# Loading the first expert's first weight pair elsewhere, and writing out its products ahead of the loop

## The chip, the cores and the metric

The kernel runs on one core of a Trainium2 chip. The time is that of one execution on the device, in microseconds (us); it is the median of several runs. A profiled execution gives the trace that all rows below come from.

Names of engines: PE is TensorE's matmuls and PEld its weight loads, DVE is VectorE, ACT is ScalarE, POOL is GpSimd, SP is SyncE, which here only issues transfers (DMAs). A "q" behind a name (PEldq, SPq) is the engine's instruction queue.

## What is computed

A decoder block on 512 tokens of 1024 channels: a Conformer convolution branch and a sliding-window attention branch, merged by gates and added to x, then a mixture of experts and a final norm. Only the mixture matters here:

```python
logits = (t @ w_router + b_router).astype(F32)
top_val, top_idx = lax.top_k(logits, TOP_K)        # 4 of 32 experts for each token
gate = jax.nn.softmax(top_val, axis=-1)
...
def expert_block(args):
    xb, e = args
    h = xb @ w_mlp1[e] + b_mlp1[e]                 # 1024 -> 2048
    glu, lin = jnp.split(h, 2, axis=-1)
    glu = jnp.minimum(glu, SWIGLU_LIMIT)
    lin = jnp.clip(lin, -SWIGLU_LIMIT, SWIGLU_LIMIT)
    a = glu * jax.nn.sigmoid(SWIGLU_ALPHA * glu) * (lin + 1)
    return a @ w_mlp2[e] + b_mlp2[e]               # 1024 -> 1024
```

The 32 experts' weights are 402 MB of float32, each read once.

## The kernel before

It has three blocks one after the other, with a barrier of all engines between them: `dense_half` (norm, projections, convolution, attention, output projection, second norm u2, router and lists), `mixture` (the experts) and `finish` (the last sum and norm).

**Places in SBUF.** `big` holds an expert's weights: `t.w1` is its first 16384 columns, eight slots of 2048 columns, one for each 128 rows of w_mlp1; two slots are a *pair*, 2 MB, and there are four pairs. `t.w2` is the rest, loaded as two halves of 2 MB. There is one place for each, no second buffer. `xT` holds the normed rows `t.u2` at the end of `dense_half`, and `t.early[0]` at the end of the mixture; between them it is not used.

**Loads in `dense_half`** (SP's queue, lines 214 to 229). When the merge is done: x (line 215), pairs 0 to 2 of expert 0 (line 219), both halves of its w2 (line 221). When the output projection is done: pair 3 (line 224), whose place held an operand of it. Then the four parts of u2 are written out to memory as they come (line 228), since the mixture gathers each expert's tokens from there, and SP waits for them (line 229).

**The expert loop.** Experts are taken from a list made on the chip: a piece is up to 96 tokens. TensorE (lines 1170 to 1178) loads the piece's token count, and branches: over 64 tokens it runs `work` with three groups of 32 tokens, else with two. In the trace expert 0 has three groups and expert 1 two. `work` does the products of slots 0 to 3 for all groups, with the finding of the tokens (`dispatch`) of the expert after the next between them, then slots 4 to 7 group by group, then the products with w2 (`down`). After the last use of a pair it raises `s_w1used`, after that of a half of w2 `s_w2used`.

SP (lines 965 to 974) loads the next expert's weights, in the order pair 0 to 3, then w2's halves. Each waits until TensorE has used the same place for the expert before: pair 0 of expert 1 can be issued only when TensorE has used pair 0 of expert 0. POOL issues the gather of an expert's tokens (`xg`, line 986) and the scatter of its result (line 1006).

**Ahead of the loop in `mixture`.** TensorE dispatches expert 0, adds the gated biases to h (line 174), dispatches expert 1 and turns expert 0's gathered tokens (line 1076). SP issues the final norm's weights (line 964).

Of the kernel before, what the change touches and what calls it, by code (L numbers as in the profile page):

```python
# [30 lines left out]
P = 128  # L31
D = 1024
SEQ = 512
TT = SEQ // P
# [12 lines left out]
E = 32  # L47
# [3 lines left out]
NG = CAP // G  # L51
K_EACH = 4
PAIRS = KB // 2
FC = 256
# [103 lines left out]
def halves(ap, n):  # L158
    return ap.rearrange("p (a n) -> p a n", n=n)
# [23 lines left out]
def dense_half(nc, t):  # L183
# [5 lines left out]
    with nc.Block() as block:  # L189

        @block.sync
        def _(sp):
# [24 lines left out]
            sp.wait_ge(t.s_merge, 2 * KB)  # L217
            for q in range(PAIRS - 1):
                sp.dma_start(t.w1[:, 2 * q:2 * q + 2, :], t.d_w1[0, q]).then_inc(t.s_w1[q], 16)
# [6 lines left out]
            for j in range(TT):  # L226
                sp.wait_ge(t.s_u2, j + 1)
                sp.dma_start(t.d_u2[j * P:(j + 1) * P, :], t.u2[:, j, :]).then_inc(t.s_u2out, 16)
            sp.wait_ge(t.s_u2out, 16 * TT)

        @block.gpsimd
# [710 lines left out]
def mixture(nc, t):  # L942
# [8 lines left out]
    with nc.Block() as block:  # L951
# [7 lines left out]
        @block.sync  # L959
        def _(sp):  # L960
            n = piece_count(sp)
            last = sp.value_load(t.lists[0:1, P + 1:P + 2], min_val=E - 1, max_val=E + MORE - 1)

            sp.dma_start(t.gfin[:, :], t.d_gfin.partition_broadcast(P)).then_inc(t.s_fin, 16)
            with sp.Fori(1, n) as i:
                e = expert_of(sp, i)
                for q in range(PAIRS):
                    sp.wait_ge(t.s_w1used, i * PAIRS + (q + 1 - PAIRS))
                    sp.dma_start(t.w1[:, 2 * q:2 * q + 2, :], t.d_w1[bass.ds(e, 1), q].rearrange("e p a n -> (e p) a n")).then_inc(t.s_w1[q], 16)
                for q in range(2):  # L970
                    sp.wait_ge(t.s_w2used, i * 2 + (q - 1))
                    sp.dma_start(t.w2[:, 2 * q:2 * q + 2, :, :],
                                 t.d_w2[bass.ds(e, 1), q].rearrange("e p j a n -> (e p) j a n")).then_inc(t.s_w2[q], 16)

            sp.wait_ge(t.s_scat, last * 16)
            for r in range(TOPK - 1):
                if r:
                    sp.wait_ge(t.s_w1used, last * PAIRS + r)
                sp.dma_start(t.early[r], t.d_y4[:, :, r, :]).then_inc(t.s_early[r], 16)
# [67 lines left out]
        def _(pe):  # L1047
# [30 lines left out]

            def up(k, g):

                for c in range(4):
                    cols = t.w1[:, k, :].rearrange("p (a n) -> p a n", a=2)[:, :, c * FC:(c + 1) * FC]
                    mm = pe.matmul(halves(bank[g][c * G:(c + 1) * G, :], FC), t.xe[:, k, PLACE[g]:PLACE[g] + G], cols,  # L1083
                                   start=(k == 0), stop=(k == KB - 1), tile_position=(0, c * G))
                return mm
# [33 lines left out]

            def work(i, groups):  # L1120

                last = groups - 1
                for k in range(K_EACH):
                    if k % 2 == 0:
                        pe.wait_ge(t.s_w1[k // 2], i * 16 + 16)
                    for g in range(groups):
                        mm = up(k, g)
                    if k % 2:
# [6 lines left out]
                for g in range(groups):  # L1135
# [3 lines left out]
                    for k in range(K_EACH, KB):  # L1139
                        if g == 0 and k % 2 == 0:  # L1140
                            pe.wait_ge(t.s_w1[k // 2], i * 16 + 16)
                        mm = up(k, g)
                        if g == last and k % 2:
# [25 lines left out]
            pe.wait_ge(t.s_acc, 2 * TT)  # L1169
            with pe.Fori(0, n) as i:  # L1170
                pe.wait_ge(t.s_xe, i * 2 + 2)
# [3 lines left out]
                with pe.If(tokens > (NG - 1) * G):  # L1175
                    work(i, NG)
                with pe.Else():
                    work(i, NG - 1)

# [155 lines left out]
def build(nc, io):  # L1335
    with ExitStack() as ctx:
# [54 lines left out]
        t.xT = halves(xT[:, :], SEQ)  # L1391
        t.u2 = halves(xT[:, :], D)
        t.early = (t.u2, halves(big[:, 0:4096], D), halves(big[:, 4096:8192], D))
        t.o_lo = halves(xT_r[:, :], SEQ)
# [258 lines left out]
```

## Time and profile before

| what | value |
|---|---|
| median of 3 runs | 1584.43 us (1584.23 to 1585.93) |
| profiled execution | 1582.41 us |
| its span, first to last instruction | 1580.6 us |
| mean granted TensorE clock | 0.967 of full speed |
| busy: PE, DVE, ACT, POOL | 90%, 47%, 36%, 22% of the span |
| moved | 475 MB, 301 GB/s on average, about 425 GB/s in the expert loop |

Times in rows are counted from the span's start. A matmul's busy time is modelled and overlaps its neighbours', so PE's 90% is not a measure of how full it is. The DMA share is the mean of the core's 16 DMA engines; 1.00 means that there was always something to move. "issue" as a releaser means that an engine waited for nothing that the profile shows.

### The profile page before, as it was taken

To read this page: it belongs to the slowest core of one execution; us is meant where nothing else is said; L and a number is where in the kernel's file an instruction comes from. 1 tells how busy PE (TensorE), PEld (TensorE's weight loads), DVE (VectorE), ACT (ScalarE), POOL (GpSimd) and SP (SyncE) were. 2 spreads that over 40 slices of the span, in tenths; PEclk is the share of its full clock that TensorE was granted. 3 is DMA by queue.
4 is the path that set the end of the run, shared out by engine and by line. 5 is a ranking of instruction groups with operands and counts; after the bars stand their busy time and mean duration, and the time that the engine had idled before them with its cause. 6 is when DMAs were issued, how large, how long until landed. Compare 5 with 4: busy or idle time off the path is not lost. (4 is left out here: it accounts for less than half of the span.)

```text
span 1580.6 us, 35484 instructions
## 1 busy us (share of the span) xinstructions
PE 1428.3 (90%) x13353; PEld 762.1 (48%) x13354; DVE 742.3 (47%) x1786; ACT 567.0 (36%) x1078; POOL 346.5 (22%) x229
## 2 busy tenths in 40 slices
PE   5999999799997689999999999999889898999991
PEld 2788776566776234433344434434333433344341
DVE  6699977899214623422233332333323422323236
ACT  3444444755223023422333332432323333224233
POOL 4578777411551000000000000000000000000000
PEclk9999999899999799999999999999999999999995
DMA  4222221111329189999999999999999999999995
GB/s 155 84 93 94 92 94 64 44 41 41 114 92 409 64 326 389 429 427 416 387 374 428 419 430 426 419 428 428 428 427 422 429 409 425 427 388 407 426 412 219
DMA packets 51665, 475.18 MB, mean 301 GB/s; under 512 B 9136, under 2 KB 9392, under 8 KB 27056
## 3 DMA queue, kind: packets, MB, share of 16 engines
q1 hardware_dynamic: 42000, 455.71, 70.4%
q0 software_dynamic: 8480, 16.79, 2.8%
q10 hardware_dynamic: 1152, 2.24, 0.4%
q8 instruction: 20, 0.33, 0.1%
q14 instruction: 13, 0.11, 0.0%
HBM read 471.56 MB, written 16.78 MB: 309 GB/s over the span
## 5 line engine op out<-in xcount | busy, mean ns | idle before, releaser
L1083 PE MATMUL bank<-big,ring 128*32 128x512 f32 x4992 | 568.1, 601 | 44.0 <-issue 22.1
L1083 PEld LDWEIGHTS bank<-big,ring 128*32 128x32 f32 x4992 | 152.3, 111 | 382.2 <-issue 347.9
L1109 PE MATMUL bank<-big,mix 128*32 128x256 f32 x4992 | 288.6, 382 | 3.9 <-DMA big<-in_d_w 3.8
L1109 PEld LDWEIGHTS bank<-big,mix 128*32 128x32 f32 x4992 | 164.1, 110 | 98.8 <-DMA big<-in_d_w 7.4
L1042 ACT ACTIVATE mix<-bank,sgate 32x256 f32<-32x256 f32 x384 | 178.7, 465 | 67.1 <-PE bank L1109 42.9
L986 POOL DMA_INDIRECT ring<-u_rows,gidx x34 | 34.4, 1010 | 580.0 <-PE bank L1076 567.0
L1030 ACT ACTIVATE ring<-ring 128x256 f32<-128x256 f32 x96 | 40.0, 416 | 312.7 <-DVE ring L1236 312.7
L474 PE MATMUL bank<-mix_r,sm_r 128*128 128x512 f32 x328 | 132.9, 405 | 17.3 <-POOL uT_r L247 10.8
L1027 ACT ACT_TABLE_LOAD x32 | 41.1, 1283 | 262.9 <-PE bank L1067 262.9
L474 PE MATMUL bank<-mix_r,ring_r 128*128 128x512 f32 x344 | 135.0, 392 | 0.0
L474 PE MATMUL bank<-uT_r,sm_r 128*128 128x512 f32 x328 | 128.7, 392 | 0.0
L719 DVE SCALAR_TENSOR_TENSOR bank<-big,chan,bank 128x512 f32<-128x512 f32 x176 | 116.6, 748 | 0.0
L1006 POOL DMA_INDIRECT y_rows<-mix,sidx x32 | 29.8, 932 | 378.0 <-ACT mix L1042 378.0
L242 POOL TENSOR_TENSOR ring_r<-ring,sm_r 128x1024 fp32r<-128x1024 f32 x41 | 100.6, 2454 | 54.0 <-ACT sm_r L316 53.2
L1201 DVE COPY slot<-bank 128x9 f32<-128x9 f32 x34 | 5.7, 169 | 203.7 <-PE bank L1059 203.7
L1247 DVE COPY mix<-bank 128x256 f32<-128x256 f32 x96 | 40.6, 423 | 116.1 <-PE bank L1095 116.1
L1234 DVE TENSOR_TENSOR ring<-bank,b 128x512 f32<-128x512 f32 x96 | 65.6, 684 | 53.3 <-PE bank L1083 52.5
L1219 DVE COPY lT<-kf 128x128 f32 x33 | 7.5, 227 | 160.5 <-PE bank L1067 155.4
L474 PEld LDWEIGHTS bank<-mix_r,sm_r 128*128 128x128 f32 x328 | 62.4, 190 | 36.4 <-issue 10.4
L474 PEld LDWEIGHTS bank<-mix_r,ring_r 128*128 128x128 f32 x344 | 65.5, 190 | 14.4 <-issue 1.4
L474 PEld LDWEIGHTS bank<-uT_r,sm_r 128*128 128x128 f32 x328 | 62.2, 190 | 13.3
L1191 DVE TENSOR_SCALAR mix<-kb,first,place 128x480 bf16<-128x480 bf16 x136 | 45.9, 401 | 22.1 <-issue 20.3
(272 smaller groups left out, 1753.2 us busy)
## 6 DMA issues: line engine op xcount, KB each, us to landing
big<-in_d_w SPq DMA_DIRECT2D x192, 2048.0 KB, 18.4
ring<-in_d_dense SPq DMA_DIRECT2D x67, 512.0 KB, 3.2
big<-y_rows SPq DMA_DIRECT2D x2, 2048.0 KB, 19.6
xT<-in_d_xT SPq DMA_DIRECT2D x4, 512.0 KB, 9.3
uT<-in_d_x SPq DMA_DIRECT2D x1, 2048.0 KB, 9.8
u_rows<-xT SPq DMA_DIRECT2D x4, 512.0 KB, 16.6
xT<-y_rows SPq DMA_DIRECT2D x1, 2048.0 KB, 12.8
xT<-y_rows SPq DMA_DIRECT2D x4, 512.0 KB, 5.4
```

What stands on the lines that cost most here:

```text
L242: pool.tensor_tensor(t.wlo[:, slot, :], t.wring[:, slot, :], hi.bitcast(F32), ALU.subtract).then_inc(t.s_wlo, 1)
L474: mm = pe.matmul(out, a, b, start=start and i == 0, stop=stop and i == 2)
L719: conv.add(dve.scalar_tensor_tensor(row if k == TAPS_V - 1 else acc, tap(k), weight(k), acc, ALU.mult, ALU.add))
L986: pool.indirect_dma_start(out=t.xg[:, :], out_offset=None, in_=t.d_u2, in_offset=bass.IndirectOffsetOnAxis(ap=t.gidx[:, 0:1], axis=0), bou ...
L1027: act.activation(t.b1[:, half * FC:(half + 1) * FC], bank[PY[half]][:, FC:], ACT.Copy).then_inc(t.s_b1, 1)
L1030: act.activation(t.sig[:, g, :], t.hb[:, g, 0:FC], ACT.Sigmoid, scale=ALPHA).then_inc(t.s_sig, 1)
L1042: out = act.activation(t.ysb[PLACE[g]:PLACE[g] + G, c * FC:(c + 1) * FC], bank[PY[g % 2]][token, 0:FC], ACT.Copy, scale=t.sgate[token, bas ...
L1083: mm = pe.matmul(halves(bank[g][c * G:(c + 1) * G, :], FC), t.xe[:, k, PLACE[g]:PLACE[g] + G], cols, start=(k == 0), stop=(k == KB - 1), t ...
L1109: mm = pe.matmul(bank[PY[g % 2]][c * G:(c + 1) * G, 0:FC], t.aT[:, g, x, b * G:(b + 1) * G], t.w2[:, b, x, c * FC:(c + 1) * FC], start=(b ...
L1191: ins = dve.tensor_scalar(t.hot[:, j, :], t.kb[:, B_SLOT:B_SLOT + HOT], t.first[:, bass.ds(i, 1)], t.place[:, j, bass.ds(e, 1)], ALU.add, ...
L1234: dve.tensor_tensor(t.hb[:, g, :], bank[g][:, :], t.b1[:, :], ALU.add).then_inc(t.s_hfree, 1)
L1247: dve.tensor_copy(t.aT[:, g, :, :], halves(bank[PT[g]][:, 0:2 * P], P)).then_inc(t.s_ae, 1)
```

## The change

Pair 0 of expert 0 is no longer loaded at line 219 with the others. It is loaded after u2 has been written out and turned, to `t.w1first`, a new name for `xT`. The place of pair 0 in `t.w1` is thereby free from the start, and SP issues pair 0 of expert 1 at once in `mixture`. The order of all other loads and what each waits for stay as they were, but the loop on SP is cut at another point: a turn now loads pairs 1 to 3 and w2 of one expert and then pair 0 of the next, whose number is read after the wait.

TensorE must read slots 0 and 1 of expert 0 from `xT`. Its expert 0 is therefore written out ahead of the loop, with both sides of its branch, and the loop runs from expert 1.

```diff
@@ dense_half, SP @@
-            for q in range(PAIRS - 1):
+            for q in range(1, PAIRS - 1):
                 sp.dma_start(t.w1[:, 2 * q:2 * q + 2, :], t.d_w1[0, q]).then_inc(t.s_w1[q], 16)
...
             sp.wait_ge(t.s_u2out, 16 * TT)
+
+            sp.wait_ge(t.s_ut, 2 * TT)
+            sp.dma_start(t.w1first[:, :, :], t.d_w1[0, 0]).then_inc(t.s_w1[0], 16)
@@ mixture, SP @@
-            with sp.Fori(1, n) as i:
+            def first_pair(i):
+
                 e = expert_of(sp, i)
-                for q in range(PAIRS):
-                    sp.wait_ge(t.s_w1used, i * PAIRS + (q + 1 - PAIRS))
+                sp.dma_start(t.w1[:, 0:2, :], t.d_w1[bass.ds(e, 1), 0].rearrange("e p a n -> (e p) a n")).then_inc(t.s_w1[0], 16)
+
+            def others(i, done):
+
+                e = expert_of(sp, i)
+                for q in range(1, PAIRS):
+                    sp.wait_ge(t.s_w1used, done * PAIRS + (q + 1))
...
                 for q in range(2):
-                    sp.wait_ge(t.s_w2used, i * 2 + (q - 1))
+                    sp.wait_ge(t.s_w2used, done * 2 + (q + 1))
...
+            sp.wait_ge(t.s_w1[0], 16)
+            first_pair(1)
+            with sp.Fori(0, last - 1) as i:
+                others(i + 1, i)
+                sp.wait_ge(t.s_w1used, i * PAIRS + (PAIRS + 1))
+                first_pair(i + 2)
+            others(last, sp.value_load(t.lists[0:1, P + 2:P + 3], min_val=E - 2, max_val=E + MORE - 2))
@@ mixture, TensorE @@
-            def up(k, g):
+            def up(k, g, first):
...
-                    cols = t.w1[:, k, :].rearrange("p (a n) -> p a n", a=2)[:, :, c * FC:(c + 1) * FC]
+                    cols = (t.w1first if first and k < 2 else t.w1)[:, k, :].rearrange("p (a n) -> p a n", a=2)[:, :, c * FC:(c + 1) * FC]
...
-            with pe.Fori(0, n) as i:
+
+            def expert(i, first=False):
+
                 pe.wait_ge(t.s_xe, i * 2 + 2)
                 pe.wait_ge(t.s_hfree, i * NG + NG)
                 pe.wait_ge(t.s_ae, i * NG + 1)
                 tokens = pe.value_load(t.lists[0:1, bass.ds(i + 2 * P, 1)], min_val=0, max_val=SEQ)
                 with pe.If(tokens > (NG - 1) * G):
-                    work(i, NG)
+                    work(i, NG, first)
                 with pe.Else():
-                    work(i, NG - 1)
+                    work(i, NG - 1, first)
+
+            expert(0, first=True)
+            with pe.Fori(1, n) as i:
+                expert(i)
```

## Rows read from the trace of the kernel before

**Rows 1.** SP's issues, timeline, 470 to 600 us (start, length, line).

```profile
474.48 1.46 SPq L219 DMA_DIRECT2D big<-in_d_w  x3
531.76 0.34 SPq L964 DMA_DIRECT2D sm<-in_d_gfin  x1
551.46 6.20 SPq L969 DMA_DIRECT2D big<-in_d_w  x2
567.59 2.05 SPq L969 DMA_DIRECT2D big<-in_d_w  x2
593.01 4.47 SPq L969 DMA_DIRECT2D big<-in_d_w  x2
```

**Rows 2.** Busy time by stretch; last three columns are PE clock, DMA share, GB/s.

```profile
480.00:490.00 10.00, 10.00 (x46) 8.28 (x45) 0.00 (x0) 2.55 (x3) 4.71 (x2) 1.00 1.03 433
518.00:532.00 14.00, 5.59 (x14) 2.22 (x12) 9.42 (x42) 0.00 (x0) 0.95 (x1) 0.62 0.00 1
565.00:568.00 3.00, 3.00 (x30) 1.01 (x30) 2.23 (x6) 0.42 (x1) 0.00 (x0) 1.00 0.00 0
592.00:594.00 2.00, 2.00 (x32) 0.84 (x28) 0.44 (x4) 0.00 (x0) 0.00 (x0) 1.00 0.28 109
760.00:780.00 20.00, 19.53 (x272) 9.06 (x268) 6.08 (x17) 6.81 (x15) 1.94 (x2) 1.00 0.89 344
```

**Rows 3.** TensorE's waits for weights (total, times, longest): 590 to 720, then 900 to 1380.

```profile
PE bank L1083 <- DMA big<-in_d_w: 0.6, 1, 0.6
...
PE bank L1083 <- DMA big<-in_d_w: 21.0, 15, 3.9
```

**Rows 4.** SP's waits, 500 to 535 us, and the last write of u2's start (L228).

```profile
SPq L189 <- DMA u_rows<-xT: 15.8, 1, 15.8
SPq L189 <- PEq L189: 11.3, 1, 11.3
...
L228 SPq DMA_DIRECT2D u_rows<-xT x4: 319/320/364, 495.5 to 502.4; - x4
```

**Rows 5.** SP's register read at line 954, 551 to 700 us (ns min/median/max).

```profile
L954 SPq TENSOR_LOAD <-lists x4: 263/271/273, 582.4 to 667.1; - x4
```

**Rows 6.** Gather of expert 0's tokens: issue, time to landing, and TensorE's turning of them.

```profile
537.31 1.17 POOL L986 DMA_INDIRECT ring<-u_rows,gidx  x1 [5.54 <-DVE gidx L1210]
...
DMA to landing us min/median/max: 4.2/4.2/4.2
...
543.06 0.86 PE L1076 MATMUL bank<-kf,ring 96*128 96x96 f32 x8
```

**Rows 7.** TensorE's timeline: last transposes of u2; start of expert 1 (idle in brackets).

```profile
503.13 1.99 PE L630 MATMUL bank<-kf,xT 128*128 128x128 f32 x16 [0.41 <-DVE mix L843]
...
586.42 6.38 PE L1083 MATMUL bank<-big,ring 128*32 128x512 f32 x32 [4.98 <-issue]
...
593.30 3.64 PE L1083 MATMUL bank<-big,ring 128*32 128x512 f32 x32
```

**Rows 8.** TensorE's branches: L1175 at 580, L1175 from 586 on, L1170 until 700.

```profile
L1175 PEldq COMPARE_BRANCH  x1: 4427/4427/4427, 580.0 to 580.0; - x1
...
L1175 PEldq COMPARE_BRANCH  x44: 77/169/228, 586.0 to 1518.6; - x44
...
L1170 PEldq COMPARE_BRANCH  x4: 213/218/252, 584.6 to 664.8; - x4
```

**Rows 9.** DMA queues: 540 to 590 us, and all queues from 590 to 1560 us.

```profile
q8 instruction: 6, 0.10, 0.9%
...
q1 hardware_dynamic: 27572, 384.64, 94.3%
q0 software_dynamic: 8018, 15.95, 4.3%
```

**Rows 10.** By stretch, expert 0 and expert 1: PE busy (count), PEld busy (count).

```profile
545.80:580.20 34.40, 34.30 (x402) 13.85 (x406) 11.85 (x38) 8.59 (x16) 1.99 (x2) 1.00 0.70 257
586.30:612.30 26.00, 25.88 (x272) 10.78 (x276) 8.91 (x30) 6.14 (x11) 1.01 (x1) 0.89 0.93 365
```

## What the change is expected to do

> **What bounds the kernel now.** I read the profiled execution (span 1580.6 us, run 1582.4 us; the median of the three timed runs is 1584.4 us, 2.0 us above it). The 40 slices of the page split it at about 516 us: the dense half ahead of it, a routing stretch to 545.9 us, then 32 turns of the expert loop. The reader is to look first at the SP queue's issues [rows 1], which say when each 2 MB weight load may start, then at the DMA share of short stretches [rows 2], which says when the transfers really ran, and last at who TensorE waits for [rows 3].
>
> In the loop a weight load is issued only when TensorE has used the same place for the expert before. So TensorE and the DMA engines hold each other: DMA-bound where TensorE waits for weights, TensorE-bound where the DMA engines lie idle. Both kinds of stretch are there. From 590 to 720 us TensorE waits 0.6 us in all for weights; from 900 to 1380 us it waits 21.0 us [rows 3]. From 760 to 780 us the DMA share is only 0.89 although six loads per expert are wanted as fast as they can go [rows 2]: there the transfers wait for TensorE. A head start of the transfers pays only if it lives through the places where they have run dry. The question for this change is what lies just behind expert 0.
>
> **The change part by part.**
>
> *Expert 0's first pair leaves the batch at 474.5 us.* 2048 KB are 2.10 MB, at 433 GB/s [rows 2] 4.84 us of transfer. The DMA engines are full there, so the rows u2 written out behind it land about 4.8 us sooner than the 518 us that SP's wait shows (502.4 us, the last issue's start, plus 15.8 us [rows 4]). The block then waits another 11.3 us for TensorE's queue, which ends on VectorE's routing arithmetic [rows 4]. Nothing waits for the earlier landing: worth 0.
>
> *The same pair is loaded behind u2's write, to xT.* It starts near 513.5 us and needs 4.84 us plus some 2 us to land: about 520.5 us. The first use is at 545.9 us [rows 10], 25 us later, and the DMA engines are idle from 518 to 532 us [rows 2]. Cost 0. The added wait for u2's transposes is met at 505 us [rows 7], before u2 has landed. Behind it SP has only the block's end, which has 11.3 us to spare.
>
> *Expert 1's first pair is issued straight after the final norm's weights*, near 532.9 us in place of 551.5 us [rows 1]: SP issues those weights at 531.76 us and then reads one register, 0.27 us [rows 5] and a few small steps. Its data move from about 534.8 to 540 us. On POOL's queue the gather of expert 0's tokens is issued at 537.3 us, and lands 4.2 us later, at 541.5 us; TensorE turns these tokens at 543.06 us [rows 6], kept until then by its own dispatch of expert 1. So 1.5 us of cover stands against roughly 1 us of shared transfer. I take 0. If the cover were gone it would cost up to 3 us; a gain isn't possible, since TensorE is not waiting for the gather.
>
> *Is the head start kept?* This is the intended gain: 2.10 MB fewer to move once experts have begun, 4.84 us at 433 GB/s. Before, pairs 0 and 1 of expert 1 are issued at 551.5 and 557.3 us, and pair 2 not until 567.6 us, when TensorE has used the place [rows 1]. From 565 to 568 us the DMA share is 0.00 [rows 2]: both pairs were in, and the engines waited. With one pair fewer they only wait longer, and pair 2 starts at 567.6 us as now. It runs dry a second time at 592 to 594 us, with a share of 0.28 [rows 2]: expert 2's first pair, issued at 593.0 us, starts on engines that are empty again. Expert 1 itself starts late for another reason (next part), not for want of weights. So the head start is given back whole before expert 2. Gain 0.
>
> *Expert 0's code is written out ahead of the loop, with both of its branches.* What does first entry cost? TensorE starts expert 1 at 586.42 us after 4.98 us of "issue" [rows 7], so it stopped at 581.44 us. The branch instruction at the end of the 96-token side (line 1175, it jumps over the 64-token side) takes 4.43 us the first time, at 580.0 us. The loop's back branch, and the branch into the 64-token side just behind it, take at most 0.25 and 0.23 us, and none of the other 44 is longer than 0.23 us [rows 8]. The instruction queue q8 carries 6 packets of some 16 KB between 540 and 590 us and none from 590 to 1560 us [rows 9]. So a long jump to code that hasn't been loaded costs 4.4 us once; running on into new code costs nothing visible (34.30 us busy of 34.40 us in expert 0 [rows 10]), and code once used stays.
>
> After the change the jump at 580 us lands behind the written-out 64-token side, where the loop begins: new code, 4.43 us as before. Expert 1 is a 64-token one, so its branch then jumps at once over the loop's own 96-token side, 402 + 406 = 808 matmuls and weight loads long [rows 10], also new. Before, this jump went to code that lay right behind what had just run, and took 0.23 us. So one more cold jump: 4.43 - 0.23 = +4.2 us, with nothing on TensorE to hide it. Bounds: 0 if the target came in with the first load, 4.43 us if all of it is exposed. I take 4.2 because two jumps over as much code are the nearest thing to two times the one row. The back branch at 612 us finds its target loaded.
>
> The Trainium skill, "Runtime: NRT & Kernel Launch", section "Instruction fetch mechanics", says that a taken branch whose target is outside a window of two pages always stalls for a fetch. By that rule before would pay three times between experts 0 and 1 (over the side, back to the head, into the other side); the row shows one payment in three, so here the measurement decides. The rule's own outcome is a rival below.
>
> *Who feels the 4.2 us?* Expert 2's loads are tied to TensorE's use of expert 1, and the DMA engines are empty at that point, so transfers and TensorE shift together; the run-dry places behind it (760 to 780 us [rows 2]) keep them tied. Almost no wait for weights stands in 590 to 720 us that could swallow it (0.6 us [rows 3]). It reaches the end one for one.
>
> *The clock.* After the stall TensorE is granted half its clock: expert 1's first 32 matmuls take 6.38 us against 3.64 us for the next 32 [rows 7], a loss of 2.74 us that is in before's time already. A longer stall can shift how long the low level lasts after the restart; bounded by the same loss again or its absence, -2.7 to +2.7 us. I take 0.
>
> *SP's reordered queue.* In the loop the register read for the first pair now stands behind its wait, 0.27 us [rows 5] and small steps, some 0.5 us later per expert. Queued transfers, or TensorE's pace, cover it everywhere but at 593 us, and TensorE hardly waits for weights there: 0, at most +0.5 us.
>
> **Sum:** 0 + 0 + 0 - 0 + 4.2 + 0 + 0 = +4.2 us: span 1584.8, run 1586.6, median 1588.6 us.
>
> **The rivals.**
>
> A. *No second cold jump, no gain*: the loop's far side comes in with the load of the first jump, or its fetch is much quicker. For it: only one such row to go by. Against it: 808 instructions lie between. Price 0 to +2: about 1584.9 us.
>
> B. *The head start is kept* (faster): if the transfers were what holds experts 1 and 2, 4.84 us fewer would come out at the end: 1579.6 us. It decides at the empty stretch 565 to 568 us; the rows speak against it, unless the second half of the loop (21.0 us of waits for weights) drew on a head start I can't see surviving.
>
> C. *Fewer long branches* (faster): if every long jump cost, going from three to two would save 4.4 us less the cover, about 1580.2 us. Against it the 44 short branches. This is what the skill's two-page rule would make of it.
>
> D. *More loads of code* (slower still): expert 4 is the first of 96 tokens in the loop and runs the loop's other side for the first time. If that isn't fetched ahead as it was for expert 0, another 4.2 us: 1592.8 us. If the loop no longer stayed loaded at its new place, each turn would pay, 31 x 4.2 = 130 us less what the waits cover; the loop's length is unchanged, so this is remote.
>
> E. *The gather is late* by more than its 1.5 us of cover and TensorE starts expert 0 later: up to +3 us beside the forecast, 1591.6 us.
>
> **How the numbers follow.** Forecast 0.58; A 0.22; B 0.06; C 0.03; D 0.07 (the remote form 0.02 of it); E 0.04. Range: A's unchanged time less a small clock gain, 1583.2 us, up to the forecast with the clock's or the gather's bad end, 1592.6 us; B, C, D lie outside. Telling a change from none takes about 0.2%, 3.2 us. Of the forecast some four in five lies above that, with D and E this makes slower 0.57; B and C, with a little clock luck, faster 0.09; the rest 0.34. The likeliest case's own range is 1587 to 1591.5 us.
>
> **What would show it.** Right: expert 0's first matmul at 545.9 us; a line-1175 branch of 4.4 us near 580 us and a second one at once behind it; expert 1 at about 590.6 us instead of 586.4 us; expert 2's first pair issued near 597 us instead of 593.0 us; a longer empty stretch before 567.6 us. Wrong: only one long branch and expert 1 at 586.4 us (A); expert 1 earlier than that (C); less than 21 us of waits for weights in 900 to 1380 us with a shorter span (B); expert 0 starting after 546.5 us (E); a long branch or a gap at expert 4 (D).

## The result, and the profile after

| | before | after |
|---|---|---|
| median | 1584.76 us (4 runs, 1584.23 to 1585.93) | 1598.25 us (4 runs, 1597.76 to 1603.56) |
| profiled execution | 1582.41 us, span 1580.6 | 1598.33 us, span 1596.5 |
| mean granted TensorE clock | 0.967 | 0.961 |

The medians lie 13.5 us apart (a ratio of 1.0085). The ratio that was estimated from all eight runs is 1.0101 (95%: 1.0086 to 1.0116), which is 16.0 us; one of the four runs after, at 1603.56 us, lies well above the others. Below, 13.5 us is the difference of the medians. Forecast was 1588.6 us (+4.2), with 1592.6 us as the end of the range. The direction was right and the size too small by a factor of three to four.

The two profiled executions differ by 15.9 us. Of these 2.6 us are there before anything that was changed runs. SP's issue of x (line 215), just ahead of the first edited line, before and then after:

```profile
474.02 0.40 SPq L215 DMA_DIRECT2D uT<-in_d_x  x1
```

```profile
476.63 0.40 SPq L215 DMA_DIRECT2D uT<-in_d_x  x1
```

The same 2.6 us stand at TensorE's first dispatch, 534.36 us before and 536.94 us after. They are not the change's: in the experiments below the short copy, with the change's `dense_half`, has that dispatch at 534.21 us, and `few_first`, with that of before, at 536.25 us. So experts are compared by their distance from that first dispatch. At expert 31 this leaves 12.4 us, and 0.9 us more come behind it.

First TensorE's branches of line 1194 (line 1175 before): at 582 us alone, the next one, the one at 708 us, and the 38 behind it. The columns are count, ns min/median/max, first and last start.

```profile
L1194 PEldq COMPARE_BRANCH  x1: 4179/4179/4179, 582.1 to 582.1; - x1
...
L1194 PEldq COMPARE_BRANCH  x4: 77/223/6286, 587.5 to 672.9; - x4
...
L1194 PEldq COMPARE_BRANCH  x1: 6805/6805/6805, 708.4 to 708.4; - x1
...
L1194 PEldq COMPARE_BRANCH  x38: 77/169/208, 753.0 to 1533.2; - x38
```

Before there was one long branch, 4.43 us [rows 8]. After there are three: 4.18, 6.29 and 6.81 us. The first is the jump at the end of expert 0's 96-token side; the second, 1.3 us behind its end, is expert 1's jump over the loop's own 96-token side; the third is at the end of expert 4, the first expert that runs that side.

TensorE's timeline round expert 0's start, expert 0's end and expert 4's end (start, length, line, count, idle before and its releaser):

```profile
547.98 5.36 PE L1100 MATMUL bank<-xT,ring 128*32 128x512 f32 x48 [1.48 <-issue]
...
578.99 4.52 PE L1126 MATMUL bank<-big,mix 128*32 128x256 f32 x80
593.98 5.39 PE L1100 MATMUL bank<-big,ring 128*32 128x512 f32 x32 [10.46 <-issue]
...
705.31 4.52 PE L1126 MATMUL bank<-big,mix 128*32 128x256 f32 x80
717.44 6.81 PE L1100 MATMUL bank<-big,ring 128*32 128x512 f32 x48 [7.61 <-issue]
```

Where expert 5 starts before, there is next to nothing:

```profile
703.34 5.36 PE L1083 MATMUL bank<-big,ring 128*32 128x512 f32 x48 [0.47 <-issue]
```

That is the whole account. At expert 1 the idle time grew from 4.98 us [rows 7] to 10.46 us, +5.5; the first 32 matmuls take 5.39 us in place of 6.38 us [rows 7], -1.0; and expert 0 had started 0.5 us nearer to the first dispatch. Sum +4.0 us. At expert 5 the idle time grew by 7.61 - 0.47 = 7.1 us and the first 48 matmuls by 6.81 - 5.36 = 1.45 us: +8.6 us. Together 12.6 us.

Each expert's start, taken at VectorE's cast of its token numbers (one each), relative to the first dispatch, after minus before, shows these two steps and, up to expert 31, nothing else of over 1 us:

| expert | 0 | 1 | 2 | 4 | 5 | 31 |
|---|---|---|---|---|---|---|
| us | -0.5 | +4.0 | +4.0 | +4.3 | +13.0 | +12.4 |

The DMA queues in 540 to 600 us, 600 to 730 us, and all of them from 730 to 1570 us (packets, MB, share of 16 engines):

```profile
q8 instruction: 8, 0.13, 1.0%
...
q8 instruction: 8, 0.13, 0.4%
...
q1 hardware_dynamic: 23978, 332.34, 94.1%
q0 software_dynamic: 6800, 13.37, 4.1%
```

Before, the instruction queue was silent from 590 us on [rows 9]. Now 8 more packets of 16 KB come between 600 and 730 us, and then none.

Busy time by stretch (length, PE, PEld, DVE, ACT, POOL, then PE clock, DMA share, GB/s): two empty stretches of the DMA engines and two of low clock.

```profile
566.60:570.60 4.00, 4.00 (x41) 1.14 (x34) 2.37 (x6) 0.42 (x1) 0.00 (x0) 1.00 0.00 0
...
596.80:601.20 4.40, 4.40 (x52) 1.44 (x48) 0.93 (x9) 0.00 (x0) 0.00 (x0) 0.92 0.00 0
587.30:597.50 10.20, 3.52 (x20) 0.93 (x24) 0.00 (x0) 0.00 (x0) 0.22 (x1) 0.50 0.73 299
713.60:720.40 6.80, 2.96 (x16) 0.82 (x20) 0.00 (x0) 0.00 (x0) 0.20 (x1) 0.50 0.99 417
```

SP's issues, 510 to 610 us:

```profile
516.95 0.33 SPq L232 DMA_DIRECT2D xT<-in_d_w  x1
534.35 0.34 SPq L967 DMA_DIRECT2D sm<-in_d_gfin  x1
535.49 0.34 SPq L971 DMA_DIRECT2D big<-in_d_w  x1
559.41 12.31 SPq L978 DMA_DIRECT2D big<-in_d_w  x3
581.99 2.06 SPq L981 DMA_DIRECT2D big<-in_d_w  x2
600.24 0.33 SPq L971 DMA_DIRECT2D big<-in_d_w  x1
```

The loads do what the change says: expert 1's first pair leaves at 535.5 us. It buys nothing. The DMA engines lie empty from 566.6 to 570.6 us, waiting for TensorE, as they did at 565 us [rows 2], and again before expert 2's first pair.

SP's waits, 500 to 535 us, and then, in the timeline, POOL's gather of expert 0's tokens and TensorE's turning of them:

```profile
SPq L189 <- PEq L189: 15.1, 1, 15.1
SPq L232 <- DMA u_rows<-xT: 9.2, 1, 9.2
```

And the timeline:

```profile
539.91 1.18 POOL L1003 DMA_INDIRECT ring<-u_rows,gidx  x1 [5.56 <-DVE gidx L1233]
...
545.64 0.86 PE L1093 MATMUL bank<-kf,ring 96*128 96x96 f32 x8
```

SP's wait for u2's write fell from 15.8 to 9.2 us and its wait for TensorE's queue grew from 11.3 to 15.1 us [rows 4]. Counted from the issue of x, u2 landed 4.2 us sooner (518.5 us before, 516.9 us after), and the second wait is 3.8 us longer: the gain goes into that wait and the new load's issue. The gather's issue and the turning are both 2.6 us later than in [rows 6], the same as the first dispatch: the gather is not late.

### The profile page after: what moved, and what is told of

Read it like the earlier page. It is cut to its first block and busy times, and to the rows that moved or that the text cites. A ratio compares the mean times of both kernels' runs of the same rounds, so it can differ in the third digit from the quotient of the medians.

```text
span 1596.5 us, 35658 instructions
## 1 busy us (share of the span) xinstructions
PE 1435.2 (90%) x13353; PEld 765.7 (48%) x13354; DVE 742.6 (47%) x1786; ACT 567.2 (36%) x1078; POOL 348.1 (22%) x229
## 5 line engine op out<-in xcount | busy, mean ns | idle before, releaser
L477 PEld LDWEIGHTS bank<-uT_r,sm_r 128*128 128x128 f32 x328 | 63.1, 192 | 13.5
## 6 DMA issues: line engine op xcount, KB each, us to landing
u_rows<-xT SPq DMA_DIRECT2D x4, 512.0 KB, 12.2
xT<-y_rows SPq DMA_DIRECT2D x1, 2048.0 KB, 12.8
```

The source lines that it names most:

```text
L477: mm = pe.matmul(out, a, b, start=start and i == 0, stop=stop and i == 2)
```

## The experiments

The theory: the loss is all in the copied TensorE code, as jumps to code that must be fetched, and in the slow clock behind them. Its rival: part of the loss is in the moved loads. Ratios are to the kernel before on the same chip, with 95% intervals; the median of before was 1584.28, 1584.03 and 1584.22 us in the three sets.

### The copy alone, the loads alone

Everything of the change's TensorE part, with the loads as before:

```diff
...
+            expert(0)
+            with pe.Fori(1, n) as i:
+                expert(i)
```

> Edit: the loads of the kernel before, every one of them; only TensorE's expert 0 is written out ahead of the loop, with both sides of its branch, reading the same places. Theory C (code entered for the first time): the whole loss is in the copy, so this kernel is slower than before by about as much as the changed kernel, +12 to +15 us, with the same long branches in the trace: about 4.2 us at the end of expert 0, about 6 us right behind it, about 6.8 us at the end of expert 4. Theory L (the moved loads cost: a later start of expert 0, transfers in the gather's way, SP's order in the loop): this kernel is within 2 us of before or at most +5 us, the one extra long jump of the prediction.

Measured: 1598.02 us, 1.0093 (1.0078 to 1.0108), +13.7 us. Branches of line 1176 (first two, then the one at 706 us) and TensorE's timeline:

```profile
L1176 PEldq COMPARE_BRANCH  x2: 4362/5333/6304, 580.1 to 585.7; - x2
...
L1176 PEldq COMPARE_BRANCH  x1: 7152/7152/7152, 706.5 to 706.5; - x1
```

TensorE's timeline:

```profile
592.16 5.52 PE L1083 MATMUL bank<-big,ring 128*32 128x512 f32 x32 [10.60 <-issue]
...
715.41 7.06 PE L1083 MATMUL bank<-big,ring 128*32 128x512 f32 x48 [7.46 <-issue]
```

The same three long branches, the same two steps in the experts' starts (+4.3 at expert 1, +13.2 at expert 5, +12.9 at expert 31), the same time as the whole change.

The loads as changed, with one loop from 0. TensorE then reads slots 0 and 1 from `xT` for every expert, so the products of experts 1 to 31 with these two slots use expert 0's weights. As `xT` is then in use to the end, part 0 of the last sum is loaded last of the three; the final norm's weights are loaded behind the loop too, and no longer ahead of it:

```diff
-                    cols = t.w1[:, k, :]...
+                    cols = (t.w1first if k < 2 else t.w1)[:, k, :]...
...
             sp.wait_ge(t.s_scat, last * 16)
-            for r in range(TOPK - 1):
+            sp.dma_start(t.gfin[:, :], t.d_gfin.partition_broadcast(P)).then_inc(t.s_fin, 16)
+            for r in (1, 2, 0):
```

> Edit: the loads of the changed kernel, but no copied code: TensorE runs all experts in the loop and reads slots 0 and 1 from the place of the normed rows for every expert, so the products of the other experts are not the reference's. The final norm's weights are loaded at the end, since two waits may not stand side by side there. Theory C: within 1 us of before, with expert 1 starting 5.0 us after expert 0's end as in before; the pair that was moved arrives early and nothing waits for it. Theory L: slower by several us. Rival B of the prediction (the head start is kept): faster by up to 4.8 us.

Measured: 1592.99 us, 1.0055 (1.0041 to 1.0069). The long branch and the idle time are those of before:

```profile
L1194 PEldq COMPARE_BRANCH  x45: 87/169/4395, 583.6 to 1520.9; - x45
```

TensorE's timeline:

```profile
590.05 5.25 PE L1100 MATMUL bank<-xT,ring 128*32 128x512 f32 x32 [5.02 <-issue]
```

Its experts 1 to 31 start -0.1 to +1.7 us from before's, expert 31 at +0.6 us. Expert 0 is 1.7 us late, as TensorE was granted half its clock in its first matmuls (48 of them took 7.05 us instead of 5.36 us), and expert 1 has made that up. Its 8.7 us lie behind the loop. To tell whether they come from the edit at the end, that edit (the last lines of the diff above) was made to the kernel before by itself:

> Edit: the kernel before with only the two changes behind the loop that the kernel of the moved loads alone had besides: the final norm's weights are loaded there, and the first of the three early parts of y is loaded last instead of first. VectorE adds that part first, so it waits for all three. Theory C: this alone explains that kernel's +8.7 us, so +8 to +10 us against before, and the moved loads cost nothing. Theory L: the tail is worth 1 us at most, and the moved loads cost the 8.7 us.

Measured: 1593.38 us, 1.0055 (1.0042 to 1.0069), the same. VectorE's wait for part 0 in the last sum, before and then here, says why:

```profile
1545.62 4.63 DVE L1288 TENSOR_TENSOR uT<-uT,xT 128x1024 f32<-128x1024 f32 x4 [0.27 <-DMA xT<-y_rows]
```

```profile
1560.61 4.63 DVE L1288 TENSOR_TENSOR uT<-uT,xT 128x1024 f32<-128x1024 f32 x4 [13.48 <-DMA xT<-y_rows]
```

So the moved loads cost and gain nothing that can be measured here: 1.0055 with them and 1.0055 without, each known to some 2 us. The theory holds, its rival falls, for TensorE's code as it is in these kernels.

### Shorter copy

The 96-token side serves any count up to 96, so for expert 0 it is written out alone, without the branch. All else as in the change:

```diff
-            expert(0, first=True)
+            pe.wait_ge(t.s_xe, 2)
+            pe.wait_ge(t.s_hfree, NG)
+            pe.wait_ge(t.s_ae, 1)
+            work(0, NG, True)
```

> Edit: the changed kernel, but expert 0 is written out with its 96-token side alone and no branch (it holds for any count up to 96). The code runs straight on from expert 0 into the loop, so the first long jump of the changed kernel goes away. Theory C: of the 10.5 us stall before expert 1 some 4.3 us go and about 6 us stay (the jump over the loop's own 96-token side). Whether the long branch at the end of expert 4 stays depends on what TensorE keeps of its code; with it the kernel is about +9 us against before, without it about 0 to +1 us. Theory L: no change against the changed kernel, +13.5 us.

Measured: 1585.62 us, 1.0011 (1.0002 to 1.0020). The branch at 580 us:

```profile
L1194 PEldq COMPARE_BRANCH  x1: 6226/6226/6226, 580.3 to 580.3; - x1
```

TensorE's timeline:

```profile
586.73 6.13 PE L1100 MATMUL bank<-big,ring 128*32 128x512 f32 x32 [6.08 <-issue]
```

No jump at expert 0's end: it runs on into the loop, and one branch is long, expert 1's over the loop's 96-token side. It costs 6.2 us, not 4.4, in this kernel too. The stall at expert 4's end is gone. Instruction packets still come at six times between 670 and 840 us, and TensorE does not stop for them: its longest idle time by "issue" there is 0.6 us. By the medians this kernel is 1.3 us behind before in place of 13.5 us: 12.2 us come back by leaving out one copy of `work` that is never run, and the branch ahead of it.

### Does code passed once stay?

The loop gets one more turn ahead of all others, whose body is the first dispatches (an outer branch, line 1160, takes it); it runs over the head and the back branch before expert 0. Semaphore counts on the other engines are shifted by a constant.

```diff
+            with pe.Fori(0, n + 1) as j:
+                with pe.If(j > 0):
+                    i = j - 1
...
+                with pe.Else():
+                    dispatch(0)
```

> Edit: the loads and the code of the kernel before, but TensorE's work ahead of the loop (the dispatches, the gated biases, the turning of expert 0's tokens) is moved into the loop as a first pass, placed behind both sides of the branch. The far end of the loop is thereby entered while TensorE waits for VectorE anyway (7.5 us idle ahead of its first dispatch in before). Semaphores that count from an earlier pass get constant offsets. Theory C: the 4.4 us branch at the end of expert 0 falls to about 0.2 us, expert 1 starts about 5 us earlier and at full clock, 2.7 us more; transfers then hold back part of these 7.7 us, so 3 to 7 us faster than before. Rival: first entry isn't what makes that branch long (any branch at that point would be), then it stays at 4.4 us and the time within 1 us of before.

Measured: 1587.62 us, 1.0022 (1.0013 to 1.0031), slower and not 3 to 7 us faster. The outer branch and the inner one (line 1166):

```profile
L1160 PEldq COMPARE_BRANCH  x33: 67/77/3403, 534.0 to 1522.8; - x33
L1166 PEldq COMPARE_BRANCH  x45: 67/169/4127, 585.7 to 1524.0; - x45
```

The back branch (line 1159), on its first run and behind the jump at 585.7 us:

```profile
L1159 PEldq COMPARE_BRANCH  x1: 228/228/228, 548.0 to 548.0; - x1
```

```profile
L1159 PEldq COMPARE_BRANCH  x1: 243/243/243, 590.0 to 590.0; - x1
```

A fetch was paid at 534 us, mostly beside TensorE's wait for VectorE: the first dispatch follows VectorE's result by 1.2 us instead of 0.2 us. Another was paid at 585.7 us, for 4.13 us. That jump leads to the back branch, which had been run 38 us earlier: code that had been run was fetched again. This contradicts the prediction's "code once used stays" directly. Between the two runs of the back branch's code, from 548.4 to 585 us, only three instruction packets of 16 KB moved.

### Telling the jump ahead

The branch at the end of the 96-token side is announced by a hint instruction at the side's start, in the kernel before, in the changed one, and in the short copy (there also the loop's first branch, from expert 0's start):

```diff
+    with nc.body(name + "_many", valid_engines=only):
+        place = pe.mark_branch_hint_location()
+        many()
+        pe.br(name + "_end").branch_hint(place)
```

> Edit: the kernel before, with one instruction more on TensorE's queue: at the start of the 96-token side the sequencer is told where the branch at that side's end will go. Theory C (code entered for the first time makes the branch long): the fetch runs while the 96-token side is computed, the branch at the end of expert 0 falls from 4.4 us to about 0.2 us, and the granted clock doesn't fall before expert 1. 5.0 us of stall and 2.7 us of slow matmuls go; transfers take some of that back, so 3 to 7 us faster than before. Rival (the branch is long for another reason, such as a full queue): it stays at 4.4 us, within 1 us of before.

> Edit: the changed kernel with the same instruction at the start of both its 96-token sides. Theory C: the branch at the end of expert 0 (4.2 us) and that at the end of expert 4 (6.8 us) fall to about 0.2 us; the jump into the loop's 64-token side for expert 1 (6.3 us) isn't told ahead and stays. Of the +13.5 us against before some 4 us at expert 0 and 9 us at expert 4 go (stall and slow clock): within 0 to +3 us of before. If the late stall at expert 4 is a cost of the loads, it stays and the kernel is still about +9 us.

> Edit: the loads of the changed kernel, expert 0 written out with its 96-token side alone, the loop's 96-token side with its end branch told ahead, and at the start of expert 0 the loop's jump into its 64-token side told ahead too. Theory C: no long branch is left, expert 1 starts right behind expert 0 and at full clock. Against the kernel before: 3 to 7 us faster, as the kernel before with the branch told ahead. If the moved load's head start is worth something once TensorE no longer stalls, this one is faster than that one by up to 4.8 us; I expect under 1 us of difference, because the DMA engines run dry at 565 us all the same.

Measured: 1582.87 us, 0.9996 (0.9987 to 1.0005); 1594.83 us, 1.0069 (1.0054 to 1.0085); 1596.79 us, 1.0073 (1.0059 to 1.0088). The announced branch, line 192, in the first:

```profile
L192 PEldq COMPARE_BRANCH  x14: 184/184/2872, 579.6 to 1491.0; - x14
```

in the second:

```profile
L192 PEldq COMPARE_BRANCH  x14: 184/184/5128, 579.4 to 1501.2; - x14
```

and the branch of line 188 (the piece's first) at 613 us in the third:

```profile
L188 PEldq COMPARE_BRANCH  x1: 11104/11104/11104, 613.0 to 613.0; - x1
```

TensorE's timeline:

```profile
624.30 6.25 PE L1118 MATMUL bank<-big,ring 128*32 128x512 f32 x32 [11.47 <-issue]
```

All three were expected within 3 us of before or up to 7 us faster; the first came out 1.2 us faster by the medians, which its interval does not tell from no change, the other two 10.8 and 12.8 us slower. The hint shortens the jump (4.43 to 2.87 us) and does not remove it: no instruction packet moves between 573.0 us and 580.1 us, so the fetch shows only 0.5 us after the branch has begun. In the kernel before, expert 1 starts 2.5 us earlier, and expert 31 by 0.2 us: the gain is given back in the loop. In the changed kernel 2.7 us are gained (+10.8 us in place of +13.5 us); the announced branch at expert 4's end takes 5.13 us in place of 6.81 us, and the one that was not announced, at 583.4 us, takes 6.73 us. In the short copy it moves the damage: the loop's first branch takes 1.17 us in place of 6.23 us, and then expert 2's branch into its side, which stays under 0.3 us in every other kernel, takes 11.1 us.

This kernel also stops where there is no branch. TensorE stands idle ahead of a dispatch inside a side, at 588.3 us for 2.52 us and in expert 8 again:

```profile
829.32 0.75 PE L1091 MATMUL bank<-bring,mix 128*128 x12 [2.74 <-issue]
```

An instruction packet moved at 826.9 us, where the kernel before moves none [rows 9]. So "running on into new code costs nothing visible" does not hold everywhere either. From expert 7 to expert 10 this kernel falls from +11.2 to +17.1 us. My reading of the three, argued only, is that what is brought ahead takes the place of code that is needed next.

### Where the loop lies

The loop's first instruction is put at position 0 or 144 of a block of code (`head_slot`), in the changed kernel. The trace shows one thing more: both kernels now enter the loop by a branch of its own (line 1201), where the changed kernel runs straight on into it.

```diff
-            with pe.Fori(1, n) as i:
+            with pe.bass.Fori(1, n, engines=OrderedEngineSet([pe.engine]), head_slot={pe.engine: 144}) as i:
```

> Edit: the changed kernel with TensorE's loop head placed at the first slot of a 16 KB block of code; nothing else differs. Open is why the branch at the end of expert 4 (6.8 us, from the loop's 96-token side to its end) is long though expert 1 had passed that end. Theory P (place): where the loop lies in the blocks decides what is still held, so the late long branch goes or changes, and the time moves by up to 9 us against the changed kernel. Theory N (number of blocks read in since): the place doesn't matter, the three long branches stay as they are and the time is within 2 us of the changed kernel, +13.5 us against before.

> Edit: as the kernel with slot 0, but the loop head at slot 144 of a block. Theory P: another time than with slot 0, by several us. Theory N: the same time within 2 us. By both: the jump over the written-out side at the end of expert 0 and the jump into the loop's 64-token side stay long.

Measured: 1602.77 us, 1.0122 (1.0106 to 1.0137), and 1598.55 us, 1.0090 (1.0071 to 1.0108). The loop's branch (line 1201) on the way in and the later ones of line 1195, at position 144:

```profile
L1201 PEldq COMPARE_BRANCH  x1: 5788/5788/5788, 587.6 to 587.6; - x1
L1195 PEldq COMPARE_BRANCH  x43: 77/169/228, 630.2 to 1535.1; - x43
```

TensorE's timeline:

```profile
599.76 1.92 PE L1101 MATMUL bank<-big,ring 128*32 128x512 f32 x5 [15.26 <-issue]
```

At 144 the stall at expert 4's end is gone: none of 43 branches behind 630 us is longer than 0.23 us. The added branch into the loop costs 5.79 us, and expert 1 waits 15.26 us. At 0 the added branch costs 5.95 us and expert 1 waits 15.39 us, and the stall at expert 4's end is there, 6.36 us at expert 5. The two kernels differ in the position alone: which jumps are paid depends on where the code lies, not only on how much of it there is. Against the changed kernel neither is a clean comparison, as both have the added branch.

### The 64-token side first

Expert 0's jump over the other side is avoided if the 64-token side is written first. In the kernel before and in the short copy:

```diff
-                with pe.If(tokens > (NG - 1) * G):
-                    work(i, NG)
-                with pe.Else():
+                with pe.If(tokens < (NG - 1) * G + 1):
                     work(i, NG - 1)
+                with pe.Else():
+                    work(i, NG)
```

> Edit: the kernel before with the two sides of TensorE's branch in the other order, the 64-token side first. Theory C: expert 0 (96 tokens) now has to jump at its start, at 545.7 us, over code that hasn't been read: a branch of about 4.4 us, of which the 2.0 us for which TensorE waits there in before hide a part. At its end it runs straight on, so the 5.0 us stall and the slow matmuls behind it (2.7 us) go. Net 1 to 6 us faster, less what transfers take back. Rival: the new jump costs as much as the old one, clock included: within 1 us of before.

> Edit: the changed kernel with expert 0 written out as its 96-token side alone, and the loop's 64-token side first. Expert 0 to expert 1 has no jump at all; expert 1's end jumps over the loop's 96-token side (unread), and expert 4 jumps into it (unread). Theory C: no stall before expert 1, 4 to 6 us before expert 2 and 4 to 7 us before expert 4: in all +3 to +6 us against before. If the head start of the moved load was only waiting for expert 1 to start on time, it is at least 4 us faster than this sum: -1 to +2 us.

Measured: 1587.22 us, 1.0024 (1.0015 to 1.0033), and 1582.20 us, 0.9989 (0.9980 to 0.9998). The branch at expert 0's start in the first:

```profile
L1175 PEldq COMPARE_BRANCH  x1: 4724/4724/4724, 547.6 to 547.6; - x1
```

TensorE's timeline:

```profile
552.45 7.00 PE L1083 MATMUL bank<-big,ring 128*32 128x512 f32 x48 [6.63 <-issue]
```

That is the first kernel; the second's timeline at expert 2's start:

```profile
614.23 5.40 PE L1100 MATMUL bank<-big,ring 128*32 128x512 f32 x32 [6.46 <-issue]
```

The first was expected up to 6 us faster, or level; it is 3.0 us slower by the medians. The jump only moved to expert 0's start, which is 6.3 us later; expert 1 is 1.0 us and expert 31 1.8 us later than before. In the second all three parts meet: expert 0 in a straight line, then the loop's 64-token side in a straight line (expert 1 starts 4.9 us earlier than before, and SP issues expert 2's first pair at 587.5 us instead of 593.0 us [rows 1]), and one jump of 6.04 us at 606.3 us, ahead of expert 2. It has the lowest ratio of all, 2.0 us ahead of before; that is less than the 3.2 us that a comparison of two kernels was said to resolve, but its own interval, from 21 and 11 runs, just leaves out 1 (and overlaps with that of `hinted_before`). Expert 31 is 4.2 us ahead counted from the first dispatch, and 1.8 us counted from the span's start, as the first dispatch stands at 536.74 us; all four kernels measured in that set have it at 536.0 to 537.5 us.

The forecast for this kernel was +3 to +6 us if the jumps alone count, and -1 to +2 us if the moved load's head start is worth something once expert 1 starts on time. Measured is -2.0 us. The 4 to 7 us priced for the way into the 96-token side at expert 4 did not come (no branch but the one at 606.3 us is over 0.3 us long), which is enough to bring the first sum down to the measured value. But the head start is not ruled out here: from 560 to 735 us TensorE waits for no weights in this kernel, and 4.0 us in `few_first`, which has the loads of before. This TensorE code with the loads of before would have told, and was not run.

### All runs together

Sum of the branches over 0.3 us from 530 us on, time at the low clock between 560 and 900 us, and the measured ratio:

| kernel | long branches, us | low clock, us | ratio |
|---|---|---|---|
| before | 4.43 | 6.8 | 1 |
| hinted_before | 3.28 | 3.4 | 0.9996 |
| short_few_first | 6.04 | 6.8 | 0.9989 |
| short_copy | 6.23 | 6.8 | 1.0011 |
| warm_loop | 7.53 (3.4 hidden) | 3.4 | 1.0022 |
| few_first | 4.72 | 0 (6.8 ahead of 560) | 1.0024 |
| hinted_short | 13.06 | 23.9 | 1.0073 |
| hinted_after | 14.89 | 13.7 | 1.0069 |
| after_slot144 | 15.22 | 20.5 | 1.0090 |
| copy_alone | 17.82 | 17.1 | 1.0093 |
| after | 17.27 | 17.1 | 1.0101 |
| after_slot0 | 21.40 | 23.9 | 1.0122 |

The two kernels with the edit at the end are left out; their loss has another cause. The others stand nearly in the order of their long branches. From before to after there are 17.27 - 4.43 = 12.8 us more of them and 13.5 us more of time by the medians (16.0 us by the ratio); from before to after_slot0, 17.0 us, and 18.6 us by the medians (19.3 us by the ratio), with 17.1 us more at the low clock. The 5.3 us that hinted_short stood idle without a branch are not in its row.

## Why the prediction was right or wrong

*Pair 0 leaves the batch, is loaded to xT, and expert 1's first pair goes early: 0.* Right. Expert 0's first matmul stands at 547.98 us, 2.1 us later than before's 545.9 us and 0.5 us nearer to the first dispatch; the kernel with the loads alone starts expert 1 within 0.6 us of before.

*SP's waits behind u2.* Right: u2 landed 4.2 us sooner (4.8 us was expected), and the wait for TensorE's queue took it up.

*The head start is not kept.* Right, and for the reason named: the DMA engines are empty from 566.6 to 570.6 us. The kernel with the loads alone gains nothing against the one with its edit at the end alone (1.0055 each). So rival B did not happen in the change as made; whether a head start is worth something once expert 1 starts on time stays open, as said at the 64-token side.

*The gather.* Right: no change. Rival E did not happen, though its sign, expert 0 starting after 546.5 us, was met at 547.98 us: that is the 2.6 us by which everything in this execution is late. The range's upper end, 1592.6 us, was given as the clock's or the gather's bad end; their 2.7 and 3 us lead to 1591.3 and 1591.6 us, and the rest has no term.

*SP's reordered queue.* Right: expert 31 stands at +12.4 us, expert 5 at +13.0 us; nothing is added along the loop.

*A stall shifts everything one for one.* Right, and it carried the whole miss to the end. TensorE's waits for weights in 600 to 735 us and in 916 to 1396 us are

```profile
PE bank L1100 <- DMA big<-in_d_w: 1.0, 1, 1.0
...
PE bank L1100 <- DMA big<-in_d_w: 21.5, 14, 3.9
```

against 0.6 and 21.0 us [rows 3]: no wait gave way.

*The first cold jump, 4.43 us as before.* Right: 4.18 us.

*A second cold jump at once behind it, 4.2 us.* It came, at the place named; the prediction's rivals A and C did not. As a price it was mis-sized: 6.29 us, and 6.30, 6.23 us in the copy alone and the short copy. I took one row as the price of every cold jump. The net of the place, +4.0 us, agrees with the forecast's +4.2 by compensation: 1.9 us more for the jump, 1.0 us less for the first matmuls at the low clock, 0.5 us less at expert 0's start, and small steps.

*"Code once used stays"; after the second jump nothing more is fetched.* This is the step that failed, and it holds two thirds of the loss. It was read from 44 short branches [rows 8] and a silent queue [rows 9]. Both are facts of a loop that had settled and had no copy of its body ahead of it; they do not say what is kept while the code that is run is larger than the loop. The written-out expert 0 doubles that code. The warm turn shows that code run 38 us ahead can be gone, and the changed kernel that the jump at the end of the first 96-token expert in the loop costs 6.81 us, although its target, the loop's end, had last been run 37 us earlier, at 671.5 us, as the back branch of line 1200 shows:

```profile
L1200 PEldq COMPARE_BRANCH  x3: 213/223/243, 618.9 to 671.5; - x3
```

*Rival D* named expert 4 and "another 4.2 us" at a chance of 0.07. The expert was right, the place within it not: entering the side was free (0.077 us at 672.9 us, the shortest of the four above; that side lies straight ahead), leaving it was not. Priced by the row that it turned out to have and with the clock it would have been 6.8 + 1.4 = 8.2 us, and the case 1588.6 + 8.2 = 1596.8 us. It should have had a far higher chance: the argument against a first-use price there was the same row that I had just used for having one at expert 0.

*The clock, 0, at most 2.7 us either way.* Right in sum for the first stall (-1.0 us), and missing for the one at expert 5 (+1.45 us). The low level holds for 10.2 us after the first stall and 6.8 us after the second, against 6.8 us in all before; each time TensorE had stood idle just before.

The Trainium skill, "Runtime: NRT & Kernel Launch", section "Instruction fetch mechanics", says that a taken branch whose target is not in the current window of two pages forces a fetch, and names 2048 instructions as what TensorE can hold. The runs agree with neither alone. Of the 44 short branches [rows 8], 13 take 77 ns and run straight on into the 96-token side; the other 31 jump over a whole side, take 0.23 us at most, and no instruction packet moves from 590 us on [rows 9], so more than two pages are kept. The second figure fits the settled loop, whose body has some 1360 matmuls and weight loads (808 + 548 [rows 10]). With a copy ahead of it, some 2700 in all, jumps are paid that the one body doesn't pay. But the warm turn had its jump fetched again after only three packets, which the second figure alone does not explain. The section also says that kernels prefer full unrolling where possible; no run here writes the loop out in full, and writing out its first turn cost 13.5 us.

What stays open: the exact rule by which code is kept. That place and amount matter is shown; which block gives way to which isn't. At expert 4 the short copy has three packets in the 96-token side just as the changed kernel has (674.9 to 699.8 us, and 676.9 to 703.5 us), and only the changed kernel pays at the side's end. It is open too why a fetched jump costs 4.1 to 4.7 us at one place and 5.1 to 7.2 us at another.

## What to carry to other kernels

Writing out the first turn of a long loop is not free in the engine's instructions: count every jump into code that hasn't just been run, in the copy and in the loop, the ends of both sides of each branch as well as their starts, and price each at the longest such row, with the slow restart of TensorE behind it. A settled loop's short branches say nothing of the turns in which it settles. A head start of transfers was worth nothing here, where the transfers ran dry soon after, waiting for their consumer; look for the first empty stretch behind the place before building anything for it.

## What the runs showed of the hardware

- A jump to code that must be fetched, with no hint, took 4.1 to 7.2 us of TensorE's queue (3.4 us once, ahead of the first dispatch); 11.1 us once, in a kernel with hints, with the DMA engines full (share 1.03). In that kernel TensorE also stood idle for 2.52 and 2.74 us inside straight code.
- A jump's target that had been run 38 us (the extra turn) or 37 us (expert 4's end) earlier was fetched again.
- A hint at the start of a straight stretch of 808 matmuls and weight loads took 1.6 us off such a jump; no instruction packet moved between 573.0 us and 580.1 us, 0.5 us after the branch had begun.
- Moving the loop's first instruction from position 144 to position 0 of its block, with no other edit, moved the time from 1.0090 to 1.0122 of before (4.2 us by the medians), and brought back a stall of 6.36 us at expert 5.
- After each long stall TensorE was granted half its clock (0.50, that is 1.2 of 2.4 GHz) for 3.4 us (behind 3.60 us idle) up to 20.5 us (behind 15.26 us idle). Its first 32 matmuls then took 5.0 to 6.4 us against 3.64 us at the full clock [rows 7].
